# Convolution state and tail rows turned in 32x32 blocks on VectorE, with loads and stores in four bands of partitions

## The chip, the cores and the metric

The kernel runs on one core of one Trainium2 chip. The metric is the device time of one execution in microseconds (us). Three runs of the kernel before took 1546.91, 1547.6 and 1549.56 us; their median is 1547.6 us.

## The reference, cut to what matters

One inference step of a decoder layer: a mixer (an HGRN2 part and a Mamba-2 part behind one input projection) and then a mixture of experts, for a prompt of 256 tokens and, with the same weights, for 8 sequences of 4 new tokens each. The change concerns the causal convolution of width 4 in front of the Mamba-2 part. It runs over 3072 channels and needs the three rows ahead of each sequence: zeros for the prompt, the input `state_conv` (8 sequences x 3 rows x 3072 channels) for the new tokens. The last three rows of each sequence are outputs.

```
CONV_K = 4
CONV_DIM = SSD_INNER + 2 * SSD_GROUPS * SSD_STATE      # 3072

def causal_dwconv(u, prev, w, b):
    L = u.shape[1]
    full = jnp.concatenate([prev.astype(u.dtype), u], axis=1)
    out = b + w[0] * full[:, 0:L]
    for j in range(1, CONV_K):
        out = out + w[j] * full[:, j:j + L]
    return out, full[:, -(CONV_K - 1):]

q, fr, iv, g, z, xbc, dt, gate_a, gate_b = _split_cols(x @ w_in, IN_SPLITS)
xbc, conv_new = causal_dwconv(xbc, conv_prev, conv_w, conv_b)
```

## The kernel before, in words

The program is a row of blocks; at the end of each block all five engines meet, and none starts the next block before the others have arrived. The change lies in the first block, which ends 129 us into the span. The mixer goes on until about 612 us, and the experts take the rest.

The first block computes the 3072 convolution channels as 24 tiles of 128 channels, with channels on the partitions and 288 tokens (256 and 32) on the free axis. TensorE turns the tokens (`turn`), then multiplies each weight tile by them (the loop over k, then `columns`); the weights come in chunks of 2 MB into the two buffers `ring`, issued by SyncE's queue (SP), each when TensorE has finished with the chunk two before it. ScalarE copies each finished tile from PSUM into `xrow` and counts `s_me`; VectorE computes the four taps of the convolution (`convolve`) and counts `s_conv`; ScalarE applies silu and counts `s_silu`. The tiles use four PSUM banks in turn, so that the product of tile n waits until tile n-4 has been copied. ScalarE copies tile c only after it has applied silu to tile c-3, from the fourth tile on.

`state_conv` is loaded by ScalarE's queue into `prev`, one of the 24 rows (sequence, row) on each of 24 partitions (L275). TensorE turns it in 24 transposes of 24x128 into two PSUM banks (L402), after the vectors (L397, L398) and ahead of `columns(0, 1)`. VectorE copies it from there into the gaps of `xrow` in two halves (L314), and only then starts the first convolution. Ahead of it on VectorE is the copy of the vectors (L310).

After the last convolution VectorE gathers the last three rows of each sequence in `ncol` (L339, L340), 27 columns (3 of the prompt, 24 of the samples) for each channel tile. TensorE, now working through four tiles of the next chunk (L432), turns them in two groups of 12 transposes (`tail`, L425), one after the second and one after the third of these tiles. VectorE copies each group from PSUM into `nrows` (L350), one row on each of 27 partitions. SP waits for both copies, stores `nrows` with two DMAs (L218, L219) and waits until they have landed (`s_out`), before it arrives at the end of the block.

The order of the work is written out by hand, engine by engine, with semaphores.

Of the kernel before, what the change touches and what calls it, by code (L numbers as in the profile page):

```python
# [21 lines left out]
P = 128  # L22
# [67 lines left out]
def build(nc, x_prompt, x_sample, state_hgrn, state_ssm, state_conv, hg_lower_bounds, w_in, hg_norm_w, hg_proj,  # L90
# [24 lines left out]
    with ctx:  # L115
# [37 lines left out]
        alog = at("alog", 101.75, [P, SH])  # L153
        dskr = at("dskr", 101.875, [P, SH])
        xrow = at("xrow", 32, [P, CT, CROW])
        prev = at("prev", 62, [NB * 3, XBC])
        ncol = at("ncol", 74, [P, CT, 27])
        nrows = at("nrows", 80, [27, XBC])
        acc = [at(f"acc{i}", 92 + 1.25 * i, [P, CROW]) for i in range(2)]
        vrows = [at("vrows0", 94.5, [P, P]), at("vrows1", 95, [24, P])]  # L160
        wdt = at("wdt", 103, [P, KD, SH])
# [13 lines left out]
        s_xte = S1("xT_copied")  # L175
        s_vt = S1("vectors_transposed")
        s_ve = S1("vectors_copied")
        s_pt = S1("conv_state_transposed")
        s_pe_ = S1("conv_state_copied")
        s_mt = S1("projection_ready")  # L180
# [7 lines left out]
        s_dtp = S1("dt_ready")  # L188
        s_nc = S1("conv_tail_gathered")
        s_nct = S1("conv_tail_transposed")  # L190
        s_nce = S1("conv_tail_copied")
        s_out = S("outputs_stored")
        s_par = S("ssd_parameters_loaded")

# [4 lines left out]
        with nc.Block() as block:  # L199
            @block.sync  # L200
            def _(sp):
                sp.dma_start(xtok[:, 0, :], x_prompt[0, 0:P, :]).then_inc(s_in, 16)
                sp.dma_start(xtok[0:32, 2, :], x_sample.rearrange("b s d -> (b s) d")).then_inc(s_in, 16)
                for i in range(4):
                    sp.dma_start(ring[0][:, 2 * i:2 * i + 2, :], w_k[:, 2 * i:2 * i + 2, C_X:C_X + CW]).then_inc(s_first[i] if i < 3 else s_w[0], 16)
                sp.dma_start(ring[1][:], chunk_src(C_X + CW)).then_inc(s_w[1], 16)
                with sp.Fori(1, 3) as i:
                    for n in range(2):

                        sp.wait_ge(s_mt, i * 8 + (4 * n - 4))  # L210
                        sp.dma_start(ring[n][:], chunk_src(i * (2 * CW) + (C_X + n * CW))).then_inc(s_w[n], 16)
                for n in range(2):

                    sp.wait_ge(s_mt, CT - 4 + 4 * n)
                    sp.dma_start(ring[n][:], chunk_src(C_F + n * CW)).then_inc(s_w[n], 16)

                sp.wait_ge(s_nce, 2)
                sp.dma_start(o_conv_p[0, 0], nrows[0:3, :]).then_inc(s_out, 16)  # L218
                sp.dma_start(o_conv_s[0].rearrange("b r c -> (b r) c"), nrows[3:27, :]).then_inc(s_out, 16)  # L219
                sp.wait_ge(s_out, 32)  # L220

            @block.gpsimd
            def _(pool):
# [7 lines left out]
                    last = g.tensor_copy(id4s[band, :], ident[band, band])  # L231
                last.then_inc(s_ones, 1)
                pool.wait_ge(s_ones, 2)
                g.memset(xrow[:, :, 0:3], 0.0).then_inc(s_zero, 1)
                g.memset(dt[:], 0.0).then_inc(s_zero, 1)
                pstep(g.memset(keep[:], 1.0))
# [27 lines left out]
            @block.scalar  # L264
            def _(act):
                a = nc.scalar
                vr = vrows[0]
                act.dma_start(xtok[:, 1, :], x_prompt[0, P:2 * P, :]).then_inc(s_in, 16)
                act.wait_ge(s_in, 48)
                act.dma_start(vr[0:96, :], conv_w[0].rearrange("j (c p) -> (j c) p", p=P)).then_inc(s_vec, 16)  # L270
                act.dma_start(vr[96:120, :], conv_b[0].rearrange("(c p) -> c p", p=P)).then_inc(s_vec, 16)
                act.dma_start(vr[120:128, :], hg_norm_w[0].rearrange("(c p) -> c p", p=P)).then_inc(s_vec, 16)
                act.dma_start(vrows[1][0:16, :], ssd_norm_w[0].rearrange("(c p) -> c p", p=P)).then_inc(s_vec, 16)
                act.dma_start(vrows[1][16:24, :], hg_lower_bounds[0].rearrange("(c p) -> c p", p=P)).then_inc(s_vec, 16)
                act.dma_start(prev[:], state_conv[0].rearrange("b r c -> (b r) c")).then_inc(s_prev, 16)  # L275
                act.dma_start(wdt[:], w_k[:, :, C_DT:C_DT + SH]).then_inc(s_wdt, 16)
                act.dma_start(dtb[:], row(dt_bias[0])).then_inc(s_wdt, 16)
                act.dma_start(alog[:], row(a_log[0])).then_inc(s_par, 16)
                act.dma_start(dskr[:], row(d_skip[0])).then_inc(s_par, 16)
                for c in range(CT + 2):  # L280
                    if c < CT:
                        act.wait_ge(s_mt, c + 1)
                        a.copy(xrow[:, c, 3:3 + SEQ], ps[:, 4 + c % 4, 0:SEQ])
                        a.copy(xrow[:, c, FROW:CROW].rearrange("p (b s) -> p b s", s=7)[:, :, 3:7],
                               ps[:, 4 + c % 4, SEQ:T].rearrange("p (b s) -> p b s", s=NS)).then_inc(s_me, 1)
                    if c == 8:
                        act.wait_ge(s_dtq, 1)
                        a.copy(dtc[:], ps[:, 3, 0:T]).then_inc(s_dtc, 1)
                    if c >= 2:
                        k = c - 2  # L290
                        act.wait_ge(s_conv, k + 1)
                        out = convX[:, k, :] if k < XT_ else convBC[:, k - XT_, :]
                        a.activation(out[:, 0:SEQ], acc[k % 2][:, 0:SEQ], ACT.Silu)
                        a.activation(out[:, SEQ:T].rearrange("p (b s) -> p b s", s=NS),
                                     acc[k % 2][:, FROW:CROW].rearrange("p (b s) -> p b s", s=7)[:, :, 0:NS],
                                     ACT.Silu).then_inc(s_silu, 1)

                for j in range(4):
                    act.wait_ge(s_mt, CT + j + 1)
                    a.copy(eT[:, j, :], ps[:, 4 + j, 0:T]).then_inc(s_me, 1)  # L300

            @block.vector
            def _(dve):
# [5 lines left out]
                dve.wait_ge(s_vt, 1)  # L309
                v.tensor_copy(vecs[:, 0:152], ps[:, 2, 0:152]).then_inc(s_ve, 1)  # L310
                dve.wait_ge(s_zero, 1)
                for h in range(2):
                    dve.wait_ge(s_pt, h + 1)
                    v.tensor_copy(xrow[:, 12 * h:12 * h + 12, FROW:CROW].rearrange("p c (b s) -> p c b s", s=7)[:, :, :, 0:3],  # L314
                                  ps[:, h, 0:288].rearrange("p (c b s) -> p c b s", b=NB, s=3)).then_inc(s_pe_, 1)
                dve.wait_ge(s_ve, 1)
                dve.wait_ge(s_pe_, 2)

                def convolve(i, n, first=False):

# [15 lines left out]
                with turns(dve, 1, CT // 2, (dstep, 6)) as i:  # L336
# [2 lines left out]
                v.tensor_copy(ncol[:, :, 0:3], xrow[:, :, SEQ:FROW]).then_inc(s_nc, 1)  # L339
                v.tensor_copy(ncol[:, :, 3:27].rearrange("p c (b s) -> p c b s", s=3),  # L340
                              xrow[:, :, FROW:CROW].rearrange("p c (b s) -> p c b s", s=7)[:, :, :, 4:7]).then_inc(s_nc, 1)

                dve.wait_ge(s_dtp, 1)
                dve.wait_ge(s_wdt, 32)
                dve.wait_ge(s_zero, 2)
                for t, (_, rows) in enumerate(TILES):
                    v.tensor_tensor(dt[0:rows, t, :], ps[0:rows, 3, 32 * t:32 * t + 32], dtb[0:rows, :], ALU.add)
                for h in range(2):
                    dve.wait_ge(s_nct, h + 1)
                    v.tensor_copy(nrows[:, 1536 * h:1536 * h + 1536].rearrange("p (c n) -> p c n", n=512),  # L350
                                  ps[0:27, 0:3, :]).then_inc(s_nce, 1)

            @block.tensor
            def _(pe):
# [41 lines left out]
                pe.wait_ge(s_vec, 80)  # L396
                m.transpose(ps[:, 2, 0:P], vrows[0][:], ident[:])  # L397
                m.transpose(ps[:, 2, P:P + 24], vrows[1][:], ident[0:24, 0:24]).then_inc(s_vt, 1)  # L398
                pe.wait_ge(s_prev, 16)
                for h in range(2):  # L400
                    for c in range(12):
                        last = m.transpose(ps[:, h, 24 * c:24 * c + 24], prev[:, (12 * h + c) * P:(12 * h + c + 1) * P], ident[0:24, 0:24])  # L402
                    last.then_inc(s_pt, 1)

                columns(0, 1)
                pe.wait_ge(s_wdt, 32)
# [10 lines left out]
                    last = m.matmul(ps[0:rows, 3, 32 * t:32 * t + 32], dtc[:, t0:t0 + rows], id4s[:], start=True, stop=True)  # L417
                last.then_inc(s_dtp, 1)

                def tail(h):  # L420

                    if h == 1:
                        pe.wait_ge(s_nce, 1)
                    for c in range(12):
                        last = m.transpose(ps[0:27, c // 4, (c % 4) * P:(c % 4 + 1) * P], ncol[:, 12 * h + c, :], ident[:])  # L425
                    last.then_inc(s_nct, 1)

                pe.wait_ge(s_w[0], 16 * 4)
                for j in range(4):
                    pe.wait_ge(s_me, CT - 3 + j)  # L430
                    for k in range(KD):
                        last = m.matmul(ps[:, 4 + j, 0:T], ring[0][:, k, j * P:(j + 1) * P], xT[:, k, :],  # L432
                                        start=(k == 0), stop=(k == KD - 1))
                    last.then_inc(s_mt, 1)
                    if j == 1:

                        pe.wait_ge(s_nc, 2)
                        tail(0)
                    if j == 2:
                        tail(1)  # L440

# [304 lines left out]
        with nc.Block() as block:  # L748
            @block.sync
            def _(sp):  # L750
# [66 lines left out]
                    rows = 256 if i < 4 else 512  # L817
                    sp.dma_start(dst[:], src[0, bass.ds(e, 1), r:r + rows, :].rearrange("a (p k) n -> p (a k) n", p=P)).then_inc(sem, 16)

                sp.wait_ge(s_out, 96)  # L820
                for t in range(2):
                    sp.dma_start(xres[:, t, :], x_prompt[0, P * t:P * t + P, :]).then_inc(g_xr, 16)
                sp.dma_start(xres[0:32, 2, :], x_sample.rearrange("b s d -> (b s) d")).then_inc(g_xr, 16)
# [78 lines left out]
                for t in range(2):  # L902
# [3 lines left out]
                    if t == 0:  # L906
                        y_s = y_sample.rearrange("b s d -> (b s) d")
                        for q in range(4):
                            sp.dma_start(y_s[:, 256 * q:256 * q + 256], yq[bands[q], :]).then_inc(s_out, 16)
                sp.wait_ge(s_out, 96 + 16 * 8)  # L910

            @block.gpsimd
            def _(pool):
# [1477 lines left out]
```

## Time and profile before

| | us |
|---|---|
| runs of the kernel before | 1546.91, 1547.6, 1549.56 |
| median | 1547.6 |
| span of the profiled execution, first to last instruction | 1543.3 |
| TensorE busy in the span | 1482.6 (96%) |
| VectorE busy | 490.4 (32%) |
| ScalarE busy | 277.5 (18%) |
| GpSimd busy | 110.5 (7%) |
| mean granted TensorE clock | 0.995 of full speed |

The profile gives the span of the profiled execution, and no separate total for it. The median of the runs is 4.3 us longer than the span; this is what lies before the first and after the last instruction, and differences of the one are read as differences of the other. The table is read from the top: TensorE is busy nearly all the time, so an edit elsewhere counts only where TensorE would wait for it. The transfers are the second thing to look at: from 617 us on the queues move 427 to 430 GB/s until just before the end.

### The profile page before, as it was taken

The page shows a single profiled execution, that of the slowest core. Times are in us where ns is not written, and L with a number is a line of the kernel's source. Part 1 is how long each engine was busy: PE and PEld are TensorE (multiplying, and loading weights), DVE is VectorE, ACT ScalarE, POOL GpSimd, SP SyncE. Part 2 cuts the span into 40 slices and gives each one's busy share as a digit, 9 for nine tenths or more (in the row PEclk, how much of TensorE's full clock was granted, in tenths as well). Part 3 has the DMA queues.
Part 4 walks back from the last instruction along what each step waited for, and adds up shares of the span by engine and source line. Part 5 has one row for each costly group of instructions (what it writes and reads, how often), then busy time and mean ns, then how long its engine had stood idle before and what let it go on. Part 6 is the DMA issues. An engine that isn't in the chain of part 4 may idle for free.

```text
span 1543.3 us, 21046 instructions
## 1 busy us (share of the span) xinstructions
PE 1482.6 (96%) x8238; PEld 757.0 (49%) x8239; DVE 490.4 (32%) x955; ACT 277.5 (18%) x618; POOL 110.5 (7%) x98
## 2 busy tenths in 40 slices
PE   9999999999999998999999999999999999899896
PEld 7777777655677764333333333333333333333332
DVE  3652455677350128222222122122122122122123
ACT  1222435532120004211010100101001100100102
POOL 1001222010140702000000000000000000000000
PEclk9999999999999999999999999999999999999998
DMA  6345487546339674999999999999999999999995
GB/s 208 110 163 173 149 262 235 197 137 199 120 103 315 242 298 173 427 427 428 427 428 428 429 428 428 428 428 428 428 429 429 428 428 428 430 428 428 429 428 223
DMA packets 105352, 507.67 MB, mean 329 GB/s; under 512 B 7575, under 2 KB 44031, under 8 KB 80575
## 3 DMA queue, kind: packets, MB, share of 16 engines
q1 hardware_dynamic: 100938, 499.37, 80.7%
q10 hardware_dynamic: 4360, 7.55, 1.5%
q8 instruction: 38, 0.62, 0.2%
q14 instruction: 16, 0.13, 0.0%
HBM read 491.18 MB, written 15.72 MB: 328 GB/s over the span
## 4 chain that ended last, share of the span: by engine, by line
PE 63%; DMA 25%; DVE 2%; ACT 1%; issue 1%; DVEq 0%; SPq 0%; ACTq 0%
DMA wGU<-in_w_gu 23%; PE ps L2325 11%; PE ps L2330 10%; PE ps L1829 10%; PE ps L2312 5%; PE ps L1842 4%; PE ps L2133 3%; PE ps L2147 2%; PE ps L2239 2%; PE ps L2160 2%; PE ps L2273 2%; PE ps L2247 1%; DMA ringS<-in_ssd_proj 1%; PE ps L1905 1%; ACT xs L1273 1%; PE ps L2260 1%
## 5 line engine op out<-in xcount | busy, mean ns | idle before, releaser
L2325 PE MATMUL ps<-wGU,xe 128*64 128x512 f32 x1536 | 342.2, 594 | 17.2 <-DMA wGU<-in_w_gu 16.5
L2330 PE MATMUL ps<-wD,aT 128*64 128x512 f32 x1024 | 226.8, 595 | 0.0
L2325 PEld LDWEIGHTS ps<-wGU,xe 128*64 128x64 f32 x1536 | 107.9, 137 | 232.8 <-issue 198.4
L1829 PE MATMUL ps<-xT,ring 128*128 128x288 f32 x704 | 179.6, 410 | 2.6 <-PEq L199 2.1
L1829 PEld LDWEIGHTS ps<-xT,ring 128*128 128x128 f32 x704 | 130.7, 190 | 42.4 <-issue 5.0
L2330 PEld LDWEIGHTS ps<-wD,aT 128*64 128x64 f32 x1024 | 70.7, 137 | 131.8 <-issue 127.9
L2312 PE MATMUL ps<-wGU,xe 128*64 128x512 f32 x512 | 121.3, 594 | 11.9 <-DMA wGU<-in_w_gu 11.9
L1725 DVE TENSOR_SCALAR sg<-sg 128x512 f32<-128x512 f32 x32 | 13.7, 427 | 333.9 <-ACT sg L1268 333.9
L1732 DVE COPY ysb<-ps 64x512 f32<-64x512 f32 x32 | 22.2, 694 | 304.0 <-PE ps L2334 304.0
L1268 ACT ACTIVATE sg<-ps 128x512 f32<-128x512 f32 x32 | 19.1, 597 | 469.6 <-PE ps L2317 469.6
L391 PE MATMUL ps<-xT,ring 128*128 128x288 f32 x320 | 78.1, 407 | 0.0
L2312 PEld LDWEIGHTS ps<-wGU,xe 128*64 128x64 f32 x512 | 36.4, 136 | 81.5 <-issue 78.4
L391 PEld LDWEIGHTS ps<-xT,ring 128*128 128x128 f32 x320 | 60.6, 190 | 17.1 <-issue 0.5
L2133 PE MATMUL ps<-ynT,ringS 128*128 128x288 f32 x256 | 62.5, 406 | 0.1
L2273 PE MATMUL ps<-ysb,gT 128*128 128x512 f32 x128 | 59.5, 606 | 0.0
L1842 PE MATMUL ps<-ring,xT 128*128 128x512 f32 x128 | 58.3, 600 | 0.0
L1280 ACT COPY ysb<-ps 64x512 f32<-64x512 f32 x32 | 18.5, 578 | 212.9 <-PE ps L2334 212.9
L2133 PEld LDWEIGHTS ps<-ynT,ringS 128*128 128x128 f32 x256 | 48.6, 190 | 13.9 <-DMA ringS<-in_ssd_proj 0.5
L2239 PE MATMUL ps<-hp,psel 128*64 128x512 bf16 x396 | 48.6, 378 | 0.2 <-DVE hp L1687 0.2
L1708 DVE TENSOR_TENSOR yacc<-yacc,ps 128x512 f32<-128x512 f32 x60 | 41.3, 688 | 21.9 <-PE ps L2273 21.9
L2273 PEld LDWEIGHTS ps<-ysb,gT 128*128 128x128 f32 x128 | 22.9, 189 | 35.1 <-issue 35.1
L1842 PEld LDWEIGHTS ps<-ring,xT 128*128 128x128 f32 x128 | 23.3, 190 | 25.7 <-issue 25.3
(476 smaller groups left out, 1451.0 us busy)
## 6 DMA issues: line engine op xcount, KB each, us to landing
wGU<-in_w_gu SPq DMA_DIRECT2D x128, 2048.0 KB, 36.7
wD<-in_w_down SPq DMA_DIRECT2D x64, 2048.0 KB, 36.8
ring<-in_w_in SPq DMA_DIRECT2D x21, 2048.0 KB, 8.8
out<-hst SPq DMA_DIRECT2D x8, 1024.0 KB, 5.8
ringS<-in_ssd_proj SPq DMA_DIRECT2D x4, 2048.0 KB, 10.0
wbuf<-prompt_A_rows ACTq DMA_DIRECT2D x16, 384.0 KB, 3.9
out<-Sb SPq DMA_DIRECT2D x2, 2048.0 KB
ring<-in_hg_proj SPq DMA_DIRECT2D x2, 2048.0 KB, 8.7
```

What stands on the lines that cost most here:

```text
L391: last = m.matmul(ps[:, 4 + mt, 0:T], ring[n][:, k, mt * P:(mt + 1) * P], xT[:, k, :], start=(k == 0), stop=(k == KD - 1))
L1708: v.tensor_tensor(y, y, p, ALU.add).then_inc(m_sa, 1)
L1829: last = m.matmul(ps[:, b, 0:T], ring[c % 2][:, k, n * P:(n + 1) * P], xT[:, k, :], start=(k == 0), stop=(k == KD - 1))
L1842: last = m.matmul(ps[:, b, :], xT[:, k, t0:t0 + rows], ring[c % 2][:, k, :], start=(k == 0), stop=(k == KD - 1))
L2133: last = m.matmul(ps[:, 7 - c % 2, 0:T], ringS[n % 2][:, k, (c % 2) * P:(c % 2) * P + P], ynT[:, k, :], start=(k == 0), stop=(k == XT_ - 1))
L2147: last = m.matmul(ps[:, 4 + c % 2, 0:T], ring[n][:, k, (c % 4) * P:(c % 4) * P + P], onT[:, k, :], start=(k == 0), stop=(k == HH - 1))
L2160: last = m.matmul(ps[:, b, :], mT[:, k, t0:t0 + rows], ring[n][:, k, :], start=(k == 0), stop=(k == KD - 1))
L2239: last = m.matmul(ps[half[h], B_X, :], psel[:, t, :], hp0[t][i][:, CW * h:CW * h + CW], start=False, stop=(t == 1 and i == 2))
L2273: return m.matmul(ps[:, bank, :], gT[:, t * P:(t + 1) * P], ysb[j % 2][:], start=True, stop=True)
L2312: last = m.matmul(ps[half[h], bank, :], xe[:, 2 + k, 1, :], wgu[n][:, k, col + CW * h:col + CW * h + CW], start=False, stop=False)
L2325: last = m.matmul(ps[half[h], bank, :], xe[:, f, hx, :], wgu[n][:, k, col + CW * h:col + CW * h + CW], start=(i == 0 and k == 0), stop=False)
L2330: last = m.matmul(ps[half[h], B_Y, :], aT[:, k, i - 4, :], wdn[n][:, k, CW * h:CW * h + CW], start=(i == 4 and k == 0), stop=False)
```

## The change

`prev` becomes a tile of 128 partitions, 24 channel tiles and 32 channels. Each channel tile of 128 is cut into four bands of 32, and band j lies on the partitions 32j to 32j+23, one for each of the 24 rows. GpSimd clears the tile first, since eight partitions of each band stay empty. ScalarE's queue loads it with four DMAs in place of one. The contiguous piece of such a DMA is 32 channels, that is 128 bytes, where it was a row of 12,288 bytes. VectorE transposes the whole tile in blocks of 32x32 (`prevT`), and copies from there into `xrow` in one instruction. TensorE has no part in it.

At the end of the block `ncol` has 32 columns in place of 27; VectorE clears the last five, transposes the tile in 32x32 blocks into `nrows` (now 128 partitions), and SP stores it with eight DMAs in place of two, again in pieces of 128 bytes. The two `tail` groups of TensorE and the two copies from PSUM are gone. The later waits on `s_out` count the six more DMAs.

```diff
-        prev = at("prev", 62, [NB * 3, XBC])
-        ncol = at("ncol", 74, [P, CT, 27])
-        nrows = at("nrows", 80, [27, XBC])
+        prev = at("prev", 62, [P, CT, 32])
+        prevT = at("prevT", 65, [P, CT, 32])
+        ncol = at("ncol", 74, [P, CT, 32])
+        nrows = at("nrows", 80, [P, CT, 32])
...
-                sp.wait_ge(s_nce, 2)
-                sp.dma_start(o_conv_p[0, 0], nrows[0:3, :]).then_inc(s_out, 16)
-                sp.dma_start(o_conv_s[0].rearrange("b r c -> (b r) c"), nrows[3:27, :]).then_inc(s_out, 16)
-                sp.wait_ge(s_out, 32)
+                sp.wait_ge(s_nct, 1)
+                for j in range(4):
+                    sp.dma_start(o_conv_s[0].rearrange("b r (c j m) -> j (b r) c m", j=4, m=32)[j], nrows[32 * j + 3:32 * j + 27, :, :]).then_inc(s_out, 16)
+                    sp.dma_start(o_conv_p[0, 0].rearrange("r (c j m) -> j r c m", j=4, m=32)[j], nrows[32 * j:32 * j + 3, :, :]).then_inc(s_out, 16)
+                sp.wait_ge(s_out, 128)
...
                 pool.wait_ge(s_ones, 2)
+                g.memset(prev[:], 0.0).then_inc(s_pz, 1)
...
-                act.dma_start(prev[:], state_conv[0].rearrange("b r c -> (b r) c")).then_inc(s_prev, 16)
+                act.wait_ge(s_pz, 1)
+                for j in range(4):
+                    act.dma_start(prev[32 * j:32 * j + 24, :, :], state_conv[0].rearrange("b r (c j m) -> j (b r) c m", j=4, m=32)[j]).then_inc(s_prev, 16)
...
-                for h in range(2):
-                    dve.wait_ge(s_pt, h + 1)
-                    v.tensor_copy(xrow[:, 12 * h:12 * h + 12, FROW:CROW]..., ps[:, h, 0:288]...).then_inc(s_pe_, 1)
+                dve.wait_ge(s_prev, 64)
+                v.transpose(prevT[:].rearrange("p c r -> p (c r)"), prev[:].rearrange("p c m -> p (c m)")).then_inc(s_pt, 1)
+                dve.wait_ge(s_pt, 1)
+                v.tensor_copy(xrow[:, :, FROW:CROW]..., prevT[:, :, 0:24]...).then_inc(s_pe_, 1)
...
+                v.memset(ncol[:, :, 27:32], 0.0).then_inc(s_nc, 1)
+                dve.wait_ge(s_nc, 3)
+                v.transpose(nrows[:].rearrange("p c m -> p (c m)"), ncol[:].rearrange("p c r -> p (c r)")).then_inc(s_nct, 1)
...
-                for h in range(2):
-                    dve.wait_ge(s_nct, h + 1)
-                    v.tensor_copy(nrows[:, 1536 * h:1536 * h + 1536]..., ps[0:27, 0:3, :]).then_inc(s_nce, 1)
...
-                pe.wait_ge(s_prev, 16)
-                for h in range(2):
-                    for c in range(12):
-                        last = m.transpose(ps[:, h, 24 * c:24 * c + 24], prev[:, (12 * h + c) * P:(12 * h + c + 1) * P], ident[0:24, 0:24])
-                    last.then_inc(s_pt, 1)
...
-                    if j == 1:
-                        pe.wait_ge(s_nc, 2)
-                        tail(0)
-                    if j == 2:
-                        tail(1)
...
-                sp.wait_ge(s_out, 96)
+                sp.wait_ge(s_out, 192)
```

On VectorE, between the copy of the vectors and the first convolution, there stands before:

```order
L310 COPY vecs<-ps 128x152 [waits vectors_transposed]
L314 COPY xrow<-ps 128x12x8x3 [waits conv_state_transposed,xrow_cleared]
L314 COPY xrow<-ps 128x12x8x3 [waits conv_state_transposed]
L329 TENSOR_SCALAR acc_79<-xrow,vecs 128x312 [waits projection_copied,conv_state_copied,vectors_copied]
L330 SCALAR_TENSOR_TENSOR acc_79<-xrow,vecs,acc_79 128x312 [waits dve_step]
```

and now:

```order
L315 COPY vecs<-ps 128x152 [waits vectors_transposed]
L318 STREAM_TRANSPOSE prevT<-prev 128x768 [waits conv_state_loaded,xrow_cleared]
L320 COPY xrow<-prevT 128x24x8x3 [waits conv_state_transposed]
L335 TENSOR_SCALAR acc_80<-xrow,vecs 128x312 [waits projection_copied,conv_state_copied,vectors_copied]
L336 SCALAR_TENSOR_TENSOR acc_80<-xrow,vecs,acc_80 128x312 [waits dve_step]
```

VectorE itself now waits for the load of the state (`conv_state_loaded`), where TensorE did before.

On SP, at the end of the first block (`ring_68` is the second weight buffer, the last row is the end of the block), there stands before:

```order
L215 DMA ring_68<-in_w_in 128x8x512 [waits projection_ready]
L218 DMA out<-nrows 3x3072 [waits conv_tail_copied]
L219 DMA out<-nrows 24x3072
L199 UNCONDITIONAL_BRANCH [waits outputs_stored]
L749 UNCONDITIONAL_BRANCH [waits barrier_Pool_Activation_PE_DVE_SP_release]
```

and now:

```order
L216 DMA ring_68<-in_w_in 128x8x512 [waits projection_ready]
L220 DMA out<-nrows 576x1x32 [waits conv_tail_transposed]
L221 DMA out<-nrows 72x1x32
L220 DMA out<-nrows 576x1x32
L221 DMA out<-nrows 72x1x32
L220 DMA out<-nrows 576x1x32
L221 DMA out<-nrows 72x1x32
L220 DMA out<-nrows 576x1x32
L221 DMA out<-nrows 72x1x32
L200 UNCONDITIONAL_BRANCH [waits outputs_stored]
```

The stores no longer wait for copies that follow TensorE's transposes, and there are 4 x (576 + 72) = 2592 pieces of 32 elements in them.

## Rows read from the trace of the kernel before

**Rows 1.** The page: span, busy time of each engine, chain that ended last

```profile
span 1543.3 us, 21046 instructions
PE 1482.6 (96%) x8238; PEld 757.0 (49%) x8239; DVE 490.4 (32%) x955; ACT 277.5 (18%) x618; POOL 110.5 (7%) x98
PE 63%; DMA 25%; DVE 2%; ACT 1%; issue 1%; DVEq 0%; SPq 0%; ACTq 0%
```

**Rows 2.** Timeline of TensorE, 0 to 60 us: start, length, instruction, count

```profile
27.50 1.65 PE L402 MATMUL ps<-ident,prev 24*128 24x24 f32 x24
29.08 15.79 PE L391 MATMUL ps<-xT,ring 128*128 128x288 f32 x64
44.80 1.18 PE L409 MATMUL ps<-xT,wdt 128*32 128x288 f32 x16
```

**Rows 3.** Timeline of TensorE at the end of the first block

```profile
116.59 1.47 PE L425 MATMUL ps<-ident,ncol 128*27 128x128 f32 x12
117.90 4.05 PE L432 MATMUL ps<-xT,ring 128*128 128x288 f32 x16
...
129.19 4.12 PE L1829 MATMUL ps<-xT,ring 128*128 128x288 f32 x16 [2.06 <-PEq L199]
```

**Rows 4.** Timelines of ScalarE and SP there, and what SP waited for

```profile
127.17 0.40 ACT L300 COPY eT<-ps 128x288 f32<-128x288 f32 x1 [4.79 <-PE ps L432]
125.06 0.34 SPq L218 DMA_DIRECT2D out<-nrows  x1
125.44 0.33 SPq L219 DMA_DIRECT2D out<-nrows  x1
SPq L199 <- DMA out<-nrows: 3.0, 1, 3.0
```

**Rows 5.** Timelines of VectorE: first convolution, then end of the last one

```profile
27.69 0.32 DVE L310 COPY vecs<-ps 128x152 f32<-128x152 f32 x1 [5.84 <-PE ps L398]
29.74 0.44 DVE L329 TENSOR_SCALAR acc<-xrow,vecs 128x312 f32<-128x312 f32 x1
112.15 0.46 DVE L340 COPY ncol<-xrow 128x576 f32<-128x576 f32 x1
118.10 1.75 DVE L350 COPY nrows<-ps 27x1536 f32<-27x1536 f32 x1 [5.21 <-PE ps L425]
```

**Rows 6.** Timeline of ScalarE and its queue, 0 to 60 us

```profile
9.00 0.32 ACTq L275 DMA_DIRECT2D prev<-in_state_conv  x1
9.35 0.41 ACTq L276 DMA_DIRECT2D wdt<-in_w_in  x1
12.67 1.28 ACT L283 ACT_TABLE_LOAD   x1 [12.67 <-issue]
25.95 0.37 ACT L283 COPY xrow<-ps 128x256 f32<-128x256 f32 x1 [12.00 <-PE ps L377]
32.40 0.35 ACT L283 COPY xrow<-ps 128x256 f32<-128x256 f32 x1
```

**Rows 7.** DMA queues, 12 to 14, then 17 to 18 us: packets, MB, share

```profile
q10 hardware_dynamic: 83, 0.31, 58.4%
...
q10 hardware_dynamic: 170, 0.02, 14.8%
q1 hardware_dynamic: 167, 0.34, 93.8%
```

**Rows 8.** The same from 19.5 to 19.75 us, all packets under 512 bytes

```profile
q10 hardware_dynamic: 234, 0.03, 73.2%
```

**Rows 9.** Stretches of one us: clock; busy PE, PEld, DVE, ACT, POOL; DMA share, GB/s

```profile
115.00:116.00 1.00, 1.00 (x6) 0.79 (x5) 0.00 (x0) 0.00 (x0) 0.00 (x0) 1.00 0.20 70
...
127.00:128.00 1.00, 0.14 (x1) 0.00 (x0) 0.00 (x0) 0.40 (x1) 0.00 (x0) 1.00 0.49 147
```

**Rows 10.** Waits of SP's queue over the whole span: us in total, times, longest

```profile
SPq L818 <- PE ps L2160: 36.5, 2, 26.2
SPq L763 <- PE ps L1829: 91.4, 5, 22.5
```

More of the change, by code:

```diff
@@ L177, in build @@
         s_ve = S1("vectors_copied")
+        s_pz = S1("conv_state_rows_cleared")
         s_pt = S1("conv_state_transposed")
@@ L190, in build @@
         s_nct = S1("conv_tail_transposed")
-        s_nce = S1("conv_tail_copied")
         s_out = S("outputs_stored")
@@ L311, in _ @@
                 dve.wait_ge(s_zero, 1)
-                for h in range(2):
-                    dve.wait_ge(s_pt, h + 1)
-                    v.tensor_copy(xrow[:, 12 * h:12 * h + 12, FROW:CROW].rearrange("p c (b s) -> p c b s", s=7)[:, :, :, 0:3],
-                                  ps[:, h, 0:288].rearrange("p (c b s) -> p c b s", b=NB, s=3)).then_inc(s_pe_, 1)
+                dve.wait_ge(s_prev, 64)
+                v.transpose(prevT[:].rearrange("p c r -> p (c r)"), prev[:].rearrange("p c m -> p (c m)")).then_inc(s_pt, 1)
+                dve.wait_ge(s_pt, 1)
+                v.tensor_copy(xrow[:, :, FROW:CROW].rearrange("p c (b s) -> p c b s", s=7)[:, :, :, 0:3],
+                              prevT[:, :, 0:24].rearrange("p c (b s) -> p c b s", s=3)).then_inc(s_pe_, 1)
                 dve.wait_ge(s_ve, 1)
-                dve.wait_ge(s_pe_, 2)
+                dve.wait_ge(s_pe_, 1)
                 def convolve(i, n, first=False):
@@ L347, in _ @@
                     v.tensor_tensor(dt[0:rows, t, :], ps[0:rows, 3, 32 * t:32 * t + 32], dtb[0:rows, :], ALU.add)
-                for h in range(2):
-                    dve.wait_ge(s_nct, h + 1)
-                    v.tensor_copy(nrows[:, 1536 * h:1536 * h + 1536].rearrange("p (c n) -> p c n", n=512),
-                                  ps[0:27, 0:3, :]).then_inc(s_nce, 1)
             @block.tensor
@@ L418, in _ @@
                 last.then_inc(s_dtp, 1)
[L420 to L426, printed above, removed]
                 pe.wait_ge(s_w[0], 16 * 4)
@@ L909, in _ @@
                             sp.dma_start(y_s[:, 256 * q:256 * q + 256], yq[bands[q], :]).then_inc(s_out, 16)
-                sp.wait_ge(s_out, 96 + 16 * 8)
+                sp.wait_ge(s_out, 192 + 16 * 8)
             @block.gpsimd
```

## The prediction

> **What bounds the kernel now.** I read the page first: TensorE is busy for 96% of the span, and the chain that ended last is 63% TensorE and 25% transfers [rows 1]. The change lies in the first block. TensorE's timeline there has the end of one group at the start of the next all along [rows 2, 3], so in this block whatever TensorE has to do is on the path. Then comes the one gap that matters: TensorE stands idle for 2.06 us before L1829 at 129.19 [rows 3], at the meeting of all engines. Its last product ended at 127.13. ScalarE's last copy is over at 127.17 + 0.40 = 127.57. SP is later: it finishes issuing the two stores of `nrows` at 125.44 + 0.33 = 125.77 and then waits 3.0 us for them, until 128.8 [rows 4]. The block ends 0.4 us after that. So the end of the first block is set by the tail's chain (transposes, copy, store, landing), with TensorE and ScalarE close behind: without the store, ScalarE at 127.57 would set it, and L1829 would start at 128.0.
>
> Does a shift of this point move the end? After it every start is relative to an engine: SP issues the weights of the mixer when TensorE frees a buffer, and the experts' weights the same way (it waited for TensorE's L1829 91.4 us and for L2160 36.5 us [rows 10]). No later transfer is issued at a time of its own. I carry the shift to the end in full.
>
> **Off TensorE.** The 24 transposes of the state take from 27.50 to 29.08, where the next product starts [rows 2]: 1.58 us. A tail group takes from its start to that of the next product, 117.90 - 116.59 = 1.31 us [rows 3]; there are two such groups: 2.62 us. Sum 4.20 us, all on the path. TensorE's last product in the block then ends at 127.13 - 4.20 = 122.93, and ScalarE's copy behind it at 127.57 - 4.20 = 123.37.
>
> **The stores, out of the end of the block.** Today the copy that SP waits for follows TensorE's last transposes. Now VectorE feeds it by itself, straight after the last convolution. The convolutions are paced by TensorE, so they shift by 1.58 us: the gathering that ends at 112.15 + 0.46 = 112.61 [rows 5] ends at 111.03. I add the clearing of five columns and a wait, 0.3 us together, and the transpose. No row shows a 32x32 transpose of 128x768. The nearest are the copy of 128x576 in 0.46 us, 0.8 ns a column, and the copy of 1536 columns from PSUM in 1.75 us, 1.14 ns a column [rows 5]: 0.6 to 0.9 us, and I take 0.9; at double that, 1.8 us, it is still all hidden. `nrows` is ready at about 112.3. Eight issues at 0.33 us (as now [rows 4]) to 0.41 us (the many-piece load of `wdt` [rows 6]) make 2.6 to 3.3 us, so the last is issued by 115.7.
>
> Behind these are 2592 pieces of 128 bytes, and this is the unknown of the case. The trace has such packets as loads only. From 19.5 to 19.75 us, when nothing else moved, 234 of them went through [rows 8]: 936 a us on 16 engines, 17 ns each on an engine. The 24 rows of the samples and three of the prompt lie on few partitions. If a partition's row stays with one engine and 12 engines share the 24 rows, three engines have two sample rows and one prompt row, in each of four bands: 4 x 24 x 3 = 288 packets, at 17 ns 4.9 us. They queue behind the last weight chunk, whose packets end at 115.2 [rows 9] and will end at 113.6. So: 113.6 + 4.9 = 118.5 moved. The landing takes a little more; today the last bytes move before 128 [rows 9] and SP's wait ends at 128.8, and I take 1.1 us: 119.6. That is 3.8 us ahead of ScalarE's 123.37, so I cost the stores at nothing, with TensorE's last tiles as their cover. The cover is gone above (123.37 - 1.1 - 113.6) / 288 = 30 ns a packet. The bounds of the cost: 17 ns, as for loads, and 94 ns, what an engine takes for one pair of a small and a 2 KB packet when the queues alternate (16 engines, 170 pairs in one us [rows 7]).
>
> **The end of the block.** With ScalarE the last to arrive at 123.37 and the same 0.4 us to the start, L1829 starts at 123.8, against 129.19: a gain of 5.4 us, of which 4.2 are the transposes and 1.2 the wait for the store.
>
> **The load of the state.** It now is 2304 packets of 128 bytes in place of 24 rows, in ScalarE's queue ahead of `wdt`. ScalarE's queue and SP's take turns packet by packet (170 against 167 from 17 to 18 us [rows 7]). By the loads' two rates, 170 a us while a weight chunk is in flight and 936 alone: about 1200 packets from 12.7 us (this load moves between 12 and 14 today [rows 7]) to 19.5, the other 1100 in 1.2 to 2 us more, landed by 22 or 23. VectorE wants them when the copy of the vectors ends, 27.69 + 0.32 = 28.01 [rows 5]. Then the transpose (0.9), a wait (0.2) and a copy of 576 columns (0.46 [rows 5]) lead to 29.7, as today (29.74 [rows 5]). The convolutions start as they do now while TensorE is 1.58 us earlier. What waits for that? TensorE's fourth tile of L391 needs ScalarE's fourth copy, at 32.40 today [rows 6], 2.7 us after the first convolution starts; it needs it at 29.08 - 1.58 + 3 x 3.95 = 39.3 (15.79 / 4 = 3.95 a tile [rows 2]). So there are 6.9 us of slack. At 170 packets a us all the way the load lands at 27.3; at three quarters of that (12 of 16 engines) at 31.3, and the slack still takes it. `wdt`, behind it, would have landed by 40 in that case and is wanted at 44.80 - 1.58 = 43.2 [rows 2]. On ScalarE the three more issues cost 1.2 us ahead of a table load at 12.67, with nothing to do until 25.95 [rows 6]: nothing. GpSimd's clearing of the tile is done long before the queue is ready to load at 9.00. Cost of all this: 0, up to 2 us if the queue blocks ScalarE past 26 us.
>
> **The rivals.** *Writes dearer than 30 ns a packet, the wait for the store stays the last.* L1829 then starts at 113.6 + 288 x t + 1.1 + 0.4. At 40 ns that is 126.6, a gain of 2.6 us: 1545.0. From 49 ns on nothing is gained: SP's wait for `outputs_stored` has taken the place of the transposes. For it speaks that the stores are the one part with no likeness in the trace, and that this very wait is the last today; against it, that small reads take 17 ns and the cover is 3.8 us.
>
> *Slower: each small write costs an engine what a pair of packets does, 94 ns.* Place: SP's wait at the end of the first block. 288 x 94 ns = 27.1 us, L1829 at 142.2, 13.0 us later than today: 1560.6. It is slower by over 3.1 us from 60 ns a packet on, and up to there within 0.2%.
>
> *The state arrives late.* VectorE starts late, and beyond 36 us TensorE waits for ScalarE's fourth copy. It takes 2304 packets at under 100 a us, below anything seen; a landing at 38 us costs 2 us or so: 1544.2.
>
> *The shift isn't carried.* If later stages ran on transfers issued at fixed times, the result would be 1547.6. Against it: SP's waits [rows 10].
>
> **How the numbers follow.** Forecast 1547.6 - 5.4 = 1542.2 us, chance 0.60 (in it a gain of 4.5 to 5.8). Dear writes with a gain of 3.1 to 4.5 us, or a late state: 0.13. Dear writes or a lost shift, within 3.1 us of before: 0.14. Slower by more: 0.13. About 0.2%, 3.1 us, is what a measurement can tell from no change. Faster 0.73, same 0.14, slower 0.13. The range goes from 1540.5 (a gain of 5.8, and 1.3 for the scatter of the runs, which lie 0.7 below to 2.0 above their median) to 1547.0, which takes in write costs up to 47 ns.
>
> **What would show it.** In the profile after: the first L391 product at 27.5; the first convolution within 0.5 us of 29.7; the last product of the block ending at 122.9 and the next block starting at 123.8 with a TensorE gap of 0.9 us, not 2.06; SP's wait for `nrows` ending by 120. Wrong it is if that wait ends after 123.4, if VectorE sits waiting for `prev` beyond 29 us, or if the experts start less than 5 us earlier than before.

## The result, and the profile after

| | before | after |
|---|---|---|
| median of 20 runs each, us | 1546.78 | 1549.64 |
| lowest and highest, us | 1544.95, 1549.56 | 1547.67, 1553.85 |
| span of the profiled execution, us | 1543.3 | 1550.0 |
| instruction fetches on q8 | 38 | 76 |

The ratio of after to before is 1.0023, with a 95% interval from 1.0016 to 1.0029: the changed kernel is 2.9 us slower by the medians (3.6 by the ratio), where 5.4 us less were forecast. It is outside the range. What follows is read from one profiled execution of each. That of after took 1551.68 us, 2.0 above its median, and that of before was one of its faster ones, so the spans differ by 6.7 us and the shifts below add up to that, not to 2.9.

**The first block went as forecast.** TensorE's timeline of after, from the start of the span and at the end of the block (start, length, instruction, count; in brackets the idle time ahead and its releaser); the lines answer to [rows 2, 3]:

```profile
26.94 0.24 PE L403 MATMUL ps<-ident,vrows 24*128 24x24 f32 x1
27.11 15.79 PE L396 MATMUL ps<-xT,ring 128*128 128x288 f32 x64
...
106.75 15.79 PE L424 MATMUL ps<-xT,ring 128*128 128x288 f32 x64
123.28 2.91 PE L1815 MATMUL ps<-xT,ring 128*128 128x288 f32 x11 [0.74 <-PEq L200]
```

The next block starts at 123.28 and not at 129.19: 5.91 us earlier. VectorE's and ScalarE's timelines and SP's waits, where they answer to [rows 4 to 6]:

```profile
27.21 0.32 DVE L315 COPY vecs<-ps 128x152 f32<-128x152 f32 x1 [5.83 <-PE ps L403]
27.45 0.97 DVE L318 STREAM_TRANSPOSE prevT<-prev 128x768 f32<-128x768 f32 x1
29.01 0.44 DVE L335 TENSOR_SCALAR acc<-xrow,vecs 128x312 f32<-128x312 f32 x1
...
110.81 0.98 DVE L350 STREAM_TRANSPOSE nrows<-ncol 128x768 f32<-128x768 f32 x1
```

```profile
8.56 7.57 ACTq L280 DMA_DIRECT2D prev<-in_state_conv  x4
16.16 1.87 ACTq L281 DMA_DIRECT2D wdt<-in_w_in  x1
20.59 1.28 ACT L288 ACT_TABLE_LOAD   x1 [20.59 <-issue]
25.48 0.37 ACT L288 COPY xrow<-ps 128x256 f32<-128x256 f32 x1 [3.61 <-PE ps L382]
...
122.58 0.40 ACT L305 COPY eT<-ps 128x288 f32<-128x288 f32 x1 [3.48 <-PE ps L424]
```

```profile
111.82 1.04 SPq L220 DMA_DIRECT2D out<-nrows  x1
112.91 0.77 SPq L221 DMA_DIRECT2D out<-nrows  x1
...
117.95 0.76 SPq L221 DMA_DIRECT2D out<-nrows  x1
SPq L200 <- DMA out<-nrows: 1.4, 1, 1.4
```

The copy of the vectors starts 0.48 us earlier than in [rows 5], before any changed work on TensorE: this much of the 5.91 us is not the change's (in all twelve profiled executions it starts between 27.21 and 28.30), and 5.43 us are left, where 5.4 were forecast. SP's last issue ends at 118.71 and its wait 1.4 us later, at 120.1. ScalarE's last copy ends at 122.98 and is the last to arrive, as forecast.

**The time is lost in the experts.** The page and the waits of TensorE from 640 to 1527 us, the experts but for their start and the last block (us in total, times, longest), first before, then after. There is no such "issue" line in before:

```profile
q8 instruction: 38, 0.62, 0.2%
PE ps L2325 <- DMA wGU<-in_w_gu: 16.5, 17, 1.2
PE ps L2312 <- DMA wGU<-in_w_gu: 11.9, 9, 1.3
```

```profile
q8 instruction: 76, 1.25, 0.3%
PE ps L2311 <- DMA wGU<-in_w_gu: 11.2, 10, 1.2
PE ps L2311 <- issue: 8.2, 4, 2.4
PE ps L2298 <- DMA wGU<-in_w_gu: 7.8, 7, 1.3
PE ps L2259 <- issue: 2.9, 3, 2.1
```

Of the fetches on q8, 32 lie between 850 and 1500 us in after; before has none in that stretch. This is the DMA view of after there, packets, MB and share:

```profile
q1 hardware_dynamic: 19035, 277.23, 100.3%
q8 instruction: 32, 0.52, 0.3%
```

They are 16 KB each, and come at nine a turn of the loop (1002 to 1175 us: 9; 1175 to 1352 us: 9). TensorE runs the experts in two blocks written out and then a loop, six blocks a turn. A block ends with VectorE's copy of `ysb`, so that copy's start in each of the 32 blocks shows the shift against before: -2.5 us in blocks 0 to 7; +1.7 at block 8; +6.2 at 14, +0.2 by 17; +5.1 at 20, +1.6 by 22; +5.9 at 26, +3.6 at the last. Each step up is at a block in which the loop has just turned back. This is TensorE's timeline at such a place, before and then after:

```profile
1000.06 0.39 PE L2334 MATMUL ps<-bd,esel 96*64 96x512 bf16 x2
1000.28 3.60 PE L2325 MATMUL ps<-wGU,xe 128*64 128x512 f32 x16
1003.82 3.70 PE L2273 MATMUL ps<-ysb,gT 128*128 128x512 f32 x8
```

```profile
1001.78 0.39 PE L2320 MATMUL ps<-bd,esel 96*64 96x512 bf16 x2
1004.58 5.23 PE L2311 MATMUL ps<-wGU,xe 128*64 128x512 f32 x16 [2.41 <-issue]
1010.04 2.41 PE L2259 MATMUL ps<-ysb,gT 128*128 128x512 f32 x5 [0.24 <-issue]
```

After 1001.78 TensorE has its operands and starts 2.4 us late with nothing to wait for but its own instructions. The same sixteen products then take 5.23 us and not 3.60. The stretches of one us say why (length of the stretch; busy PE, PEld, DVE, ACT, POOL; then, third from the end, the granted clock, DMA share, GB/s):

```profile
1003.00:1004.00 1.00, 0.00 (x0) 0.00 (x0) 0.22 (x1) 0.00 (x0) 0.00 (x0) 1.00 0.92 393
1004.00:1005.00 1.00, 0.42 (x2) 0.30 (x4) 0.52 (x3) 0.00 (x0) 0.00 (x0) 0.68 1.00 426
1005.00:1006.00 1.00, 1.00 (x4) 0.24 (x2) 0.50 (x2) 0.00 (x0) 0.00 (x0) 0.50 1.00 426
```

The first 1.00 of a line, which [rows 9] calls the clock, is its length. The clock granted is 1.00 (2.4 GHz) while the engine stands idle, and 0.50 (1.2 GHz) for some 3 us right behind. So this turn costs 2.6 us of idle time, 1.6 us of half clock and a last 0.2 us of idle, 4.5 us in all. The four steps up are 4.3, 4.5, 4.5 and 3.9 us. At the first of them the clock does not fall: there TensorE stops twice, for 1.91 and 2.07 us.

TensorE stops once more where it leaves the loop, for 2.28 us (0.79 us in before, for VectorE's `ysb`), and the clock falls behind this gap too. From the last copy of `ysb` to the end of the span the shift goes from +3.6 to +6.7 us. After:

```profile
1532.93 0.64 PE L2252 MATMUL ps<-ysb,gT 128*32 128x256 f32 x8 [2.28 <-issue]
```

### The profile page after: what moved, and what is told of

The parts are those of the page before. It is cut to its first block, busy times and chain, and to the rows that moved or that the text cites. A ratio compares the mean times of both kernels' runs of the same rounds, so it can differ in the third digit from the quotient of the medians.

```text
span 1550.0 us, 20961 instructions
## 1 busy us (share of the span) xinstructions
PE 1486.9 (96%) x8191; PEld 756.4 (49%) x8191; DVE 488.6 (32%) x955; ACT 277.8 (18%) x618; POOL 111.3 (7%) x99
## 4 chain that ended last, share of the span: by engine, by line
PE 69%; DMA 18%; issue 2%; DVE 1%; ACT 1%; DVEq 0%; SPq 0%; ACTq 0%
DMA wGU<-in_w_gu 18%; PE ps L2311 14%; PE ps L2316 11%; PE ps L1815 10%; PE ps L2298 6%; PE ps L2119 4%; PE ps L1828 4%; PE ps L2259 2%; PE ps L2225 2%; PE ps L2133 2%; PE ps L2146 2%; PE ps L2233 1%; PE ps L1891 1%; ACT xs L1259 1%; PE ps L2246 1%
## 5 line engine op out<-in xcount | busy, mean ns | idle before, releaser
L1815 PE MATMUL ps<-xT,ring 128*128 128x288 f32 x704 | 181.3, 413 | 1.3 <-PEq L200 0.7
L1815 PEld LDWEIGHTS ps<-xT,ring 128*128 128x128 f32 x704 | 131.7, 191 | 41.8 <-issue 3.7
```

What stands on the lines that cost most here:

```text
L1815: last = m.matmul(ps[:, b, 0:T], ring[c % 2][:, k, n * P:(n + 1) * P], xT[:, k, :], start=(k == 0), stop=(k == KD - 1))
```

## The experiments

| kernel | start of loop | fetches | median, us | ratio to before | interval |
|---|---|---|---|---|---|
| before | 8194 | 38 | 1546.78 | 1 | |
| after | 8098 | 76 | 1549.64 | 1.0023 | 1.0016 to 1.0029 |
| after, 48 transposes at the loop | 8196 | 38 | 1542.45 | 0.9965 | 0.9953 to 0.9977 |
| after, 48 in the first block | 8197 | 38 | 1541.53 | 0.9965 | 0.9951 to 0.9978 |
| after, 43 at the loop | 8186 | 38 | 1542.03 | 0.9965 | 0.9954 to 0.9977 |
| after, 12 at the loop | 8124 | 76 | 1549.77 | 1.0024 | 1.0015 to 1.0034 |
| before, 24 at the loop | 8244 | 39 | 1546.59 | 0.9994 | 0.9985 to 1.0003 |
| before, 54 at the loop | 8304 | 77 | 1555.59 | 1.0068 | 1.0051 to 1.0085 |
| before, 62 at the loop | 8320 | 77 | 1556.26 | 1.0053 | 1.0038 to 1.0069 |
| before, 80 at the loop | 8356 | 77 | 1554.28 | 1.0047 | 1.0033 to 1.006 |
| state part alone | 8197 | 38 | 1545.1 | 0.999 | 0.9981 to 0.9999 |
| tail part alone | 8197 | 38 | 1544.24 | 0.9981 | 0.9971 to 0.9991 |

Each ratio is to runs of before made beside those of its row, whose medians were 1546.78, 1547.79, 1546.64 and 1545.92 us in the four rounds. So medians of different rows can be compared to 1 us or so only: between after and after with padding they differ by 7 to 8 us, and the ratios by 0.0058, 9 us.

**After, with 48 transposes that never run, at the loop.**

```diff
+                with pe.If(end < 1):
+                    for _ in range(48):
+                        m.transpose(ps[0:32, 3, 0:32], smask[:], ident[0:32, 0:32])
                 with pe.Fori(0, TURNS) as it:
```

> The changed kernel with 48 transposes in TensorE's program that are never executed (a branch jumps over them), just before the loop over the experts. They put the loop back to where it starts before the change (place 8196 in TensorE's program as built, 8194 before, 8098 in the changed kernel). Theory A, the loop's place in the code: the changed kernel's loop lies over one more 16 KB piece of code and is fetched anew at each turn (76 fetches on queue 8 in place of 38, TensorE idle for about 2 us at each turn back, then a low clock). Then here: about 38 fetches, no idle piece at the turns, no low clock at 1004, 1178 and 1356 us, and a time of 1541 to 1544 us, 3 to 6 us under the kernel before. Theory B, the loss comes from the change itself (small packets, the earlier start of the second block, the clock): as the changed kernel, 1549 to 1550 us.

Measured: 1542.45 us, 38 fetches. In TensorE's waits from 600 to 1550 us one "issue" line is left:

```profile
PE ps L2311 <- issue: 0.7, 1, 0.7
```

Code that is never run gives back 7 us by the medians and 9 by the ratios. Nothing else was changed, so the loss of the change lies in where TensorE's code stands.

**After, with the same 48 in the first block's loop.** The branch is of the same kind, never taken (`pe.If((i // 2) * 2 > i)`), some 8000 places ahead of the experts.

> The changed kernel with the same 48 transposes, never executed, inside the first block's loop of TensorE, so that all later code lies within 3 places of where it lies before the change. Theory A: as with the pad just before the expert loop, and if the idle 0.87 us at 347.6 us of the changed kernel is also a late fetch, 1 us or so better: 1540 to 1543 us. Theory B: 1549 to 1550 us. The branch is taken twice and costs some 0.1 us each.

Measured: 1541.53 us, the same. TensorE's timeline at the place shown above:

```profile
995.21 0.39 PE L2323 MATMUL ps<-bd,esel 96*64 96x512 bf16 x2
995.43 3.60 PE L2314 MATMUL ps<-wGU,xe 128*64 128x512 f32 x16
998.96 3.70 PE L2262 MATMUL ps<-ysb,gT 128*128 128x512 f32 x8
```

The gap and the half clock behind it are gone together. The shift of VectorE's copy of `ysb` against before is -4.86 us in the first fifteen blocks and -4.46 us in the last: the gain of the first block is carried through all experts. Like the version before it, this one beats both kernels.

**Before, with 80 transposes at the loop**: does the kernel before lose by being moved?

> The kernel before, with 80 transposes that are never executed ahead of the expert loop, so that the loop starts at place 8356, modulo 256 nearly as in the changed kernel (164 against 162). Nothing else is changed. Theory A: 76 fetches or so, an idle piece of 2 us at each turn of the loop, 6 to 9 us slower than the kernel before: 1553 to 1556 us. Theory B: the same time as before within 1 us.

Measured: 1554.28 us, 77 fetches. Its waits have the new line, as after has it:

```profile
PE ps L2325 <- issue: 11.8, 8, 2.3
```

The effect needs no part of the change.

**Before, with 24 at the loop**, a move that by the theory stays inside.

> The kernel before, with 24 such transposes: the loop starts at place 8244 and its 1677 places end at 9920, still over 7 pieces of 256. Theory A: no extra fetches and the same time as before within 1 us; a pad as such costs nothing. If any shift of the code costs, or the piece borders lie elsewhere than counted from the start of the program: slower by 6 to 9 us.

Measured: 1546.59 us, ratio 0.9994, 39 fetches. Padding as such costs nothing that the measurement can tell; the place decides.

**The state's part alone.** It has the load in four bands and the transpose on VectorE, TensorE's tail as before, and 24 transposes that never run in the first block, so that the loop stands at 8197.

```diff
-                pe.wait_ge(s_prev, 16)
-                for h in range(2):
-                    for c in range(12):
-                        last = m.transpose(ps[:, h, 24 * c:24 * c + 24], prev[:, (12 * h + c) * P:(12 * h + c + 1) * P], ident[0:24, 0:24])
-                    last.then_inc(s_pt, 1)
```

> The change's first half alone (the state loaded in four bands and transposed by VectorE; the tail is as before), with 24 transposes that are never executed in the first block, so that later code lies within 3 places of where it lies before the change. If the working of the prediction holds for the first block: TensorE 1.6 to 2.0 us earlier at the end of the block, the wait for the store of the tail as before (TensorE idle 2.06 us), so 1.6 to 2.0 us under the kernel before: 1545 to 1546 us. If the small packets of the load cost TensorE something by contention, less than that.

Measured: 1545.1 us, ratio 0.999, 1.5 us faster. The interval only just leaves out no change, and the span of its profiled execution, 1543.4 us, is no shorter than that of before. SP's wait for the store is what it was in [rows 4]:

```profile
27.90 15.79 PE L397 MATMUL ps<-xT,ring 128*128 128x288 f32 x64
...
128.02 2.18 PE L1832 MATMUL ps<-xT,ring 128*128 128x288 f32 x8 [2.06 <-PEq L201]
SPq L201 <- DMA out<-nrows: 3.0, 1, 3.0
```

**The tail's part alone**, with the state as before and the same padding.

```diff
-                    if j == 1:
-                        pe.wait_ge(s_nc, 2)
-                        tail(0)
-                    if j == 2:
-                        tail(1)
```

> The change's second half alone (the tail transposed by VectorE and stored in eight DMAs; the state as before), with the same kind of pad. By the prediction's working 2.62 us of transposes and 1.2 us of waiting for the store are gone: the next block starts 3.8 to 4.0 us earlier, 1543 to 1544 us. If the store's small packets were slow beside the matmuls, SP's wait would be the last to end and the gain under 3 us.

Measured: 1544.24 us, just outside what was expected; ratio 0.9981, 2.9 us faster, with an interval from 1.4 to 4.5 us.

```profile
29.32 15.79 PE L390 MATMUL ps<-xT,ring 128*128 128x288 f32 x64
...
125.49 4.12 PE L1818 MATMUL ps<-xT,ring 128*128 128x288 f32 x16 [0.74 <-PEq L198]
```

From the first product of the first chunk to the start of the next block it is 129.19 - 29.08 = 100.11 us before [rows 2, 3], 100.12 with the state's part alone, 96.17 with the tail's part alone and 96.17 in after. The tail is worth 3.94 us. The state's part lies ahead of that product: from the copy of the vectors to the product it is 1.39 us before (27.69 to 29.08) and -0.10 us after (27.21 to 27.11), a gain of 1.49 us. With the 0.48 us of the earlier start this is the whole 5.91 us. The first block is measured well by these starts; over the whole kernel the two parts alone gave 1.5 and 2.9 us, which agree with 1.49 and 3.94 only within their intervals.

**After, with 43 at the loop.** Pieces of 256 places counted from the program's start have a border at 8192, and this kernel starts its loop at 8186, just ahead of it.

> The changed kernel with 43 transposes that are never executed before the expert loop: it starts at place 8186, six places below 8192 = 32 x 256, and ten below that of the variant with 48. If the pieces of code are 256 places long and are counted from the start of the program as built, this loop again lies over eight pieces: 76 fetches and 1549 to 1551 us. If what matters is nearness to the old place (whatever the border), it is as with 48: 38 fetches, 1541 to 1544 us.

Measured: 1542.03 us, 38 fetches. Of the two outcomes expected, the one for a border at 8192 did not come. The border is not at 8192 as counted.

**Before, with 62 at the loop**, at the far side.

> The kernel before with 62 such transposes: the loop starts at place 8320 and ends at 9997, 13 places past 9984 = 39 x 256. If seven pieces of 256 are what fits: about 76 fetches and 1552 to 1556 us. If eight fit, or the border is elsewhere: 38 fetches and the time of the kernel before within 1 us.

Measured: 1556.26 us, a little above what was expected, and 77 fetches, as expected.

**Two places close to the borders**, which test the size of the pieces and not where they start.

> The kernel after with 12 never-run transposes ahead of TensorE's loop over the experts; counted in instructions as built, the loop's start moves from 8098 to 8124 and the loop is 1677 long. Seen so far: starts of 8186, 8197 and 8244 run with 38 instruction fetches, 8098, 8320 and 8356 with 76 to 77. Theory: the loop runs without fetches only where it lies over seven pieces of 256 instructions, which is a stretch of starts 7 x 256 - 1677 = 115 long. 8124 and 8244 are 120 apart, so 8124 must still be outside: 76 fetches, idle 'issue' stretches of 2 us at the turns of the loop, 1549 to 1551 us. Rival: a larger store or smaller pieces, with the border anywhere between 8098 and 8186: then 8124 may well fit, 38 fetches, 1542 us.

> The kernel before with 54 never-run transposes ahead of TensorE's loop over the experts, so that it starts at 8304 as built (8194 before, 8320 and 8356 in the two runs that fetched). Theory of the seven pieces: 8186 fits, so from 8186 + 115 = 8301 on nothing does: 8304 fetches, 76 to 77, 1553 to 1556 us. Rival: a stretch of starts longer than 115, then 8304 may fit: 38 fetches, 1547 us.

Measured: 1549.77 us with 76 fetches, and 1555.59 us with 77. Both went as the theory of seven pieces had it. Starts of 8186, 8194, 8196, 8197 and 8244 run clean, 8124 and below and 8304 and above do not. So the clean stretch is at least 58 long and under 180. If the code is held in pieces of 256 places, seven of them less the loop's 1677 leave a stretch of 115, and eight would leave 371.

The page "Runtime: NRT & Kernel Launch" of the Trainium skill (Instruction fetch mechanics) says that TensorE's instruction memory holds 2048 instructions, that it is filled in pieces of 256, that the cost of going over a border is mostly hidden, and that a taken branch to a target outside the current window of two such pieces has to wait for a fetch. Waits at the turns are what the runs show, and the 16 KB of a fetch agree with a piece of that page. The window of two does not agree: before turns back over 1677 places without a fetch. By the size the page gives, eight pieces would fit, and a loop of 1677 could stand anywhere: it lies over eight at most. The runs have nine fetches a turn where, by the theory, it lies over eight, and none where it lies over seven. The measurement decides: of pieces of 256, seven can be kept, not eight. Nine for a loop over eight pieces would fit a piece that is fetched ahead of the last one and has to be held too; this is argued, and no run here shows it.

The kernel with 12 transposes shows one thing more. TensorE's waits from 640 to 1527 us, and its timeline at the first turn back:

```profile
PE ps L2311 <- issue: 25.3, 8, 4.5
PE ps L2298 <- DMA wGU<-in_w_gu: 0.7, 1, 0.7
```

```profile
835.28 1.07 PE L2311 MATMUL ps<-wGU,xe 128*64 128x512 f32 x3 [2.22 <-issue]
840.73 6.13 PE L2311 MATMUL ps<-wGU,xe 128*64 128x512 f32 x13 [4.38 <-issue]
```

Here a turn costs 10 us, more than twice what it costs in after, and yet the two kernels take the same time. The waits for weights, 28.4 us in before, are down to 0.7 us. TensorE falls behind, the weights pile up, and it catches up without waiting, until the stream of 427 GB/s sets the pace again.

## Why the prediction was right and wrong

- **Off TensorE.** Right. 4.20 us were worked out. The state's transposes gave 1.49 us (1.58 forecast); the tail with the wait for its store gave 3.94 us (2.62 + 1.2 forecast).
- **VectorE's transpose.** Taken as 0.9 us, it took 0.97 and 0.98 us, 1.27 ns a column. The first convolution starts at 29.01, 0.7 us ahead of the forecast 29.7.
- **The issues of the stores.** Mis-sized: 0.33 to 0.41 us each were taken, and they took 0.76 to 1.04 us, 6.8 us for the eight. The last was over at 118.7, not 115.7. It cost nothing, since the packets no longer set the landing: 120.1, where 119.6 was forecast.
- **The packets of the stores.** No dearer than those of the loads. From 114 to 116 us 692 packets took 25.9% of 16 engines, 12 ns each; in [rows 8] 234 took 73.2% of a quarter of a us, 12.5 ns each. The row of after:

```profile
q1 hardware_dynamic: 692, 0.09, 25.9%
```

  The rivals of dear writes (30 ns and above) fall with it. So does, for these stores, the doubled cost that the prediction worked out from the read-modify-write below 512 bytes in the page "DMA: Bandwidth & Descriptors" of the Trainium skill (Specifications): by that estimate the stores would have been done at 124.5, and they were done at 120.1.
- **The load of the state.** Its cost on ScalarE was mis-sized. The three more issues were costed at 1.2 us; the four took 7.57 us, and `wdt` behind them 1.87 us in place of 0.41. ScalarE reached its table load at 20.59, 7.9 us later than in [rows 6], and was idle for another 3.61 us until TensorE's tile was ready. The cover that the prediction named (nothing to do until 25.95) held, with 3.6 us of it left. VectorE did not wait for the load. (The two slower bounds of its landing come to 26.3 and 30.8 us from the prediction's own figures, where 27.3 and 31.3 stand; nothing hung on them.)
- **Does a shift of this point move the end?** This is the step that failed: "I carry the shift to the end in full." Its reason, that every later start is relative to an engine, was right, and the kernel padded in the first block shows it: -4.8 us at the end of that block and -4.5 in the last expert block. Its ratio of 0.9965 is 5.4 us, with an interval from 3.4 to 7.6; that it meets the forecast to the tenth is luck. What the step left out is that the change also shortens TensorE's program by 96 places, and that the place of later code in it has a price: 8 us between 1541.5 and 1549.6. The prediction's own sign of being wrong came true: the experts start 2.5 us earlier than before, not 5. The rival "the shift isn't carried" had the right place and the wrong mechanism, and it ended at no change, where a new stall ends slower.
- **How it comes about in the experts.** From block 7 to the last the shift goes from -2.5 to +3.6 us, 6.1 us. TensorE's rows of that stretch have 11.1 us of new idle time and three falls of the clock of some 1.7 us, 16.2 us together; the waits for weights shrink by 9.4 us (28.4 to 19.0), and 6.8 us are left. Leaving the loop costs 3.1 us more.
- **What was lost between 124 us and the experts.** The shift was -5.9 us at 124 us and only -2.5 us in the first experts. 1.7 us of that went when the clock fell at 130 to 134 us: sixteen products of L1815 took 5.84 us (first line below), and in before 4.15 us. This fall is a matter of the execution. It is also in the profiled executions of five experiments, some of before's code and some of after's, between 129 and 140 us, and not in before and the five others. 1.3 us went at 347 us, and these belong to the change: TensorE stops within a row of transposes (second line), waiting for nothing but its own instructions. The same gap, 0.8 to 1.2 us, is in all four kernels whose mixer code lies where after has it (after alone and with 12, 43 and 48 at the loop) and in none of the other eight, the one padded in the first block among them. So a second place of the code has a price, ahead of the loop over the experts; which fetch is late there is open. The last 0.4 us go between 570 and 620 us, and why is open.

```profile
129.81 5.84 PE L1815 MATMUL ps<-xT,ring 128*128 128x288 f32 x16
348.50 0.63 PE L1986 MATMUL ps<-ident,eT 128*32 128x128 f32 x12 [0.87 <-issue]
```

- **The base of the sum.** The prediction took the 4.3 us between the median and the span as what lies outside the span. In all eleven executions profiled later it is 1.7 to 1.8 us (after: 1551.68 for a span of 1550.0). So the profiled execution of before took about 1545.0 us and was one of its faster ones, without the fall at 130. The forecast of 1542.2 did not suffer, since it was made from the median, then 1547.6 of three runs; with the 1546.78 of twenty it would have been 1541.4.

## What to carry to other kernels

An edit that adds or removes instructions ahead of a long loop moves the loop in the engine's instruction memory, and that can cost more than the edit gains: here some 8 us against 5.4. Read the count of instruction fetches and the idle time put down to "issue" before and after each edit, and compare edits with the loop at the same place (never-run code ahead of it will do). A fetch at a turn can be paid for twice, since the clock often falls behind the gap: at three of the four turns back in after, at all four with 12 transposes, at one of four in before with 54. How much of it reaches the end depends on how long the engine would have waited for its weights anyway.

## What was not expected of the hardware

- A loop of 1677 places on TensorE ran without a fetch at starts from 8186 to 8244 and with nine fetches of 16 KB a turn at 8098 and 8124 (and with as many in all from 8304 to 8356), at 2 to 7 us of idle time a turn. That the clean stretch is 115 long is the theory's figure; the runs bound it between 58 and 180.
- By the theory of seven pieces, the border before the clean stretch is off by 6 to 63 places against the count from the program's start. This stays open, as does why the start at 8124 idles 6.6 us at its first turn back and the one at 8098 some 4 us (at 1002 us 2.6).
- A DMA of many 128-byte pieces holds the queue that issues it: 0.76 us for 72 pieces as well as 0.83 us for 576. Four loads of 576 pieces, beside a weight chunk on the other queue, held theirs for 7.57 us.
